# Second attention of a two-block transformer kernel: values held in the array, probabilities scaled before they are transposed

## The chip, the cores and the metric

One core of a Trainium2 chip runs the whole program. The metric is the device time in microseconds (us), the median of several executions. The engines are PE (matrix multiply, with its weight loads listed as PEld), DVE, ACT and POOL (elementwise work) and SP (issues the weight DMAs). Each takes its own instructions strictly in the order of the program, and they meet only through semaphores.

## The reference, cut to what matters

Two transformer blocks run one after the other on 256 tokens of width 1024, all in float32. The change touches only the attention of the second block. It has four mixers of four heads each, with a head size of 64: `moba`, `nsa` (three branches: compressed, selected `slc`, windowed `win`), `diff` (`df1`, `df2`) and `swa`. With 256 tokens every one of them comes down to masked maps of 256 x 256:

```python
s = q @ k.T * scale - slope * dist          # masked, per head
p = exp(s - max) / sum                      # swa adds a sink to the sum
o = p @ v                                   # (256 x 256) @ (256 x 64)
o_nsa = g0 * o_cmp + g1 * o_slc + g2 * o_win
mix = concat([o_moba, o_nsa, o_diff, o_swa])   # 256 x 1024
x = x + rms_norm(mix @ w_out)
```

Of a map only three blocks of 128 x 128 are not masked: query block 0 with key block 0, and query block 1 with both. There are 16 maps of `slc`, `win`, `swa` and `moba`, and 8 of `diff`, which are mixed into 4 before they meet their values. `k` and `v` of nsa are shared by its heads; swa shares each of two pairs between two heads.

## The kernel before, in words

Everything runs as one long list of steps, `ORDER` (line 436), which all five engines walk; each emits its own part of a step and skips what is not its own. A stage's list is made by `weave` (line 188): the string `MIX[...]` says at each place whether the next step comes from the main work ("." takes the next slot of projections) or from one of the side jobs (a letter takes the next step of that job). The stage of this change is `MIX["maps"]` (lines 429 and 430). Its main work is fourteen projection tiles in two halves each (`gemm`, 12 matmuls of 256 columns a half) and at the end four `down` steps of the output projection `out2` (12 matmuls of 512 columns each); after it come the `tail` steps, the rest of that projection. Weights arrive as float32 and are split into a high and a low part (`split`): the high part by ACT or DVE, the low part by DVE or POOL, as the string `MADE` says.

The side jobs are made from `two` (line 366), one per pair of maps (a group: for instance `("win", 0)` is heads 0 and 1):

- `scores`: PE, both maps of the pair, into two banks of PSUM that are kept until both maps are read;
- `score` (one map): DVE adds the bias, writes the scores to an SBUF buffer of the ring `ringP` and takes the extreme of each row;
- `exp` (one map): ACT, with the row sums;
- `p_turn` (one map): PE transposes the three blocks (line 1293), ACT copies them to a buffer of `ringT`, and DVE takes the reciprocal of the row sums, times the gate for nsa (line 2139);
- `value` (one map): PE, with the transposed probabilities stationary and the 64 columns of the values moving (`apart`, line 900: two column halves of the array, each 64 output rows, side by side);
- `o_out` (one map): DVE multiplies the result by the reciprocal, row by row, into `OM2`, which holds tokens in rows and features in columns; `win` adds onto `slc`.

`cmp_value` (two steps) multiplies the compressed probabilities with their values and DVE adds them in. `OM2` is then turned into what the output projection takes, features in rows: `join` (eight steps, line 1311) has PE transpose two blocks, ACT write the high part of the operand `mi` and DVE the low part.

The banks of PSUM for side jobs form a ring of five (`B5`); a step that takes a bank waits until its last reader is through. `ringP` has 7 buffers and `ringT` 5. Free order matters: a `p_turn` of PE needs `exp` alone, and `value` needs ACT's copy of the transposed block.

Of the kernel before, what the change touches and what calls it, by code (L numbers as in the profile page):

```python
# [21 lines left out]
NUNREAD = 13  # L22
NBASE = 4
# [190 lines left out]
def segments():  # L214
# [151 lines left out]
    def two(g):  # L366

        a, b = GROUPS[g]
        return [("scores", g), ("score", a), ("exp", a), ("score", b), ("exp", b), ("p_turn", a), ("value", a), ("p_turn", b), ("o_out", a),
                ("value", b), ("o_out", b)]  # L370

    for n in range(2):
        jobs.append(two(("slc", n)) + two(("win", n)) + [("cmp_value", n), ("join", 2 + n)])
# [4 lines left out]
    for n in range(2):  # L378
        jobs.append(two(("swa", n)) + ([("join", 6), ("join", 7)] if n else []))
    for n in range(2):  # L380
        jobs.append(two(("moba", n)) + [("join", n)])
# [27 lines left out]
    def names(steps):  # L409
# [19 lines left out]
    "maps": "...a.....acbabcbc..cc.bbb.ede.eed.ecag.agcdgcggadc.b.bfcgbefdc.ab.dgfbe.dbhffbbhhhfa.ccccf.igecbeif."  # L429
            "gahf.ddib.b.bbigchijbjj..cbhcibchkhajkhcikkhcjbiijbcijkijkcijg.kjjkk.ggkkij.k.",  # L430
# [27 lines left out]
LAST_JOIN = [s for s in ORDER if s[0] == "join"][-1]  # L458
# [124 lines left out]
def program(nc, dr):  # L583
    ctx = ExitStack()
    with ctx:  # L585
# [184 lines left out]
        OM2 = fa(o, 2048).rearrange("p (c n) -> p c n", c=2); o += 2048  # L770
        PcT, VC = fa(o, 256), fa(o + 256, 256); o += 512
        ringP = [fa(o + 384 * i, 384) for i in range(7)]; o += 7 * 384
        ringT = [fa(o + 384 * i, 384) for i in range(5)]; o += 5 * 384
# [30 lines left out]
        HEAD = dict(moba=0, slc=4, win=4, df1=8, swa=12)  # L804
# [13 lines left out]
        for m, i in p_slot.items():  # L818
            p_prior[m] = at_p.get(i - 7)
        for m, i in t_slot.items():  # L820
            t_prior[m] = at_t.get(i - 5)
# [8 lines left out]
        def Pm(m):  # L830
            return ringP[p_slot[m] % 7]

        def Tm(m):
            return ringT[t_slot[m] % 5]
# [23 lines left out]
        def opened(e, u):  # L858
# [6 lines left out]
            elif PLACE[u] >= NBASE and OPENS[1] <= u < OPENS[1] + NWIDE - NBASE:  # L865
                e.wait_ge(*pe.at(LAST_JOIN))

# [14 lines left out]
        def tensor(e):  # L882
# [53 lines left out]
            for step in ORDER:  # L936
# [356 lines left out]
                elif kind == "p_turn":  # L1293
# [3 lines left out]
                    e.wait_ge(*(dve.at(("d_mix", m_[1])) if m_[0] == "df1" else act.at(("exp", m_))))  # L1297
# [3 lines left out]
                elif kind == "value":  # L1301
# [8 lines left out]
                    apart(b[:, 64:128], PT[:, 256:384], V[1], start=False).then_inc(*pe.up(step))  # L1310
                elif kind == "join":
# [4 lines left out]
                    for c in range(2):  # L1316
                        m = e.transpose(b[:, 128 * c:128 * c + 128], OM2[:, c, 128 * kt:128 * kt + 128], ident)
# [15 lines left out]
                elif kind in ("o_out", "d_out"):  # L1333
                    banks.give(("value", a[0] if kind == "o_out" else ("df1", a[0])))
# [18 lines left out]
                elif kind == "cmp_turn":  # L1353
# [4 lines left out]
                    m.then_inc(*pe.up(step))  # L1358
                elif kind == "cmp_value":
                    n, = a  # L1360
                    b = bank(step, B5)
                    e.wait_ge(*act.at("cmp_turn"))
                    e.wait_ge(*dve.at("cmp_kv"))
                    for c in range(2):
                        m = e.matmul(b[:, 128 * c:128 * c + 128], PcT[:, 128 * c:128 * c + 128], VC[:, 128 * n:128 * n + 128],
                                     start=True, stop=True)
# [3 lines left out]
        def scalar(e):  # L1370
# [3 lines left out]
            for step in ORDER:  # L1374
# [268 lines left out]
                elif kind == "p_turn":  # L1643
                    m_, = a
                    e.wait_ge(*pe.at(step))
                    if t_prior[m_]:
                        e.wait_ge(*pe.at(("value", t_prior[m_])))
                    e.activation(Tm(m_), banks.of(step)[:, 0:384], ACT.Copy).then_inc(*act.up(step))
                    banks.ended(step, act.now())
                elif kind == "d_out":  # L1650
# [3 lines left out]
                    for c in range(2):  # L1654
                        e.activation(OM2[:, c, 64 * (8 + h):64 * (8 + h) + 64], b[:, 64 * c:64 * c + 64], ACT.Square,
# [33 lines left out]
        def vector(e):  # L1689
# [10 lines left out]
            for step in ORDER:  # L1700
# [438 lines left out]
                elif kind == "p_turn" and a[0][0] != "df1":  # L2139
                    m_, = a  # L2140
                    r = stat(("r", m_), 2)
# [349 lines left out]
```

## Time and profile before

| what | value |
|---|---|
| median of 3 runs | 897.89 us (897.86 to 898.0) |
| the profiled execution | 897.94 us |
| its span, first to last instruction | 896.1 us |
| granted TensorE clock, mean | 0.999 |
| PE busy | 884.4 us (99%) |
| DVE, ACT, POOL busy | 667.4, 466.3, 200.4 us |

The profiled execution's own time is 1.8 us over its span. "Busy" counts the time in which at least one instruction of the engine runs. A row of a timeline gives the start, the busy time, the engine, what it wrote from what, shapes, and how many instructions were merged; the start of the next row less the start of this one is what the row took of PE's time. The arrow in brackets names the engine and tile whose end let the row start. The stage `maps` lies from 519.8 to about 608 us.

### The profile page before, as it was taken

The numbers are of one execution on the slowest core, as the hardware profiler recorded it, in microseconds if no ns is written. First come the engines' busy times: TensorE is split into PE (matmuls) and PEld (weight loads), VectorE is DVE, ScalarE is ACT, GpSimd is POOL, SyncE is SP. The second block draws the span as 40 slices with busy tenths as digits, with TensorE's granted clock in tenths as the row PEclk, the third lists the DMA queues.
The fourth block names the chain that finished last, engine by engine and source line by source line (L and its number), as shares of the span: only waits on it lengthen the run. The fifth ranks groups of instructions, "written<-read, shape, count | busy, mean of one in ns | idle before, by whom it ended". The sixth has DMA issues, their size and how long they took to land.

```text
span 896.1 us, 16529 instructions
## 1 busy us (share of the span) xinstructions
PE 884.4 (99%) x6641; PEld 782.7 (87%) x6641; DVE 667.4 (74%) x1253; ACT 466.3 (52%) x940; POOL 200.4 (22%) x113
## 2 busy tenths in 40 slices
PE   9999999999999999999999999999999999999997
PEld 8879999989999798888888899977888888888886
DVE  7745987586447877786666767768888788788885
ACT  7444336665344774444444657866553545543443
POOL 4123421531132120553214522230001111210100
PEclk9999999999999999999999999999999999999999
DMA  8356453153424746555564374215354465465441
GB/s 331 114 184 234 140 174 112 48 212 142 142 96 145 278 163 236 188 196 187 187 219 169 124 247 165 97 48 211 142 222 161 182 213 204 152 230 188 174 156 48
DMA packets 23180, 153.66 MB, mean 171 GB/s; under 512 B 2864, under 2 KB 3248, under 8 KB 5568
## 3 DMA queue, kind: packets, MB, share of 16 engines
q1 hardware_dynamic: 22384, 150.44, 46.8%
q0 software_dynamic: 576, 2.10, 0.6%
q8 instruction: 53, 0.87, 0.4%
q14 instruction: 23, 0.19, 0.1%
q10 hardware_dynamic: 144, 0.07, 0.0%
HBM read 151.28 MB, written 1.05 MB: 170 GB/s over the span
## 4 chain that ended last, share of the span: by engine, by line
PE 96%; DVE 2%; ACT 1%; issue 1%; DVEq 0%; ACTq 0%
PE pb L528 94%; PE pb L531 2%; ACT FA L534 1%; DVE FA L537 0%; DVE wl L537 0%; ACT R L534 0%; DVE X L543 0%; DVE wh L552 0%; DVE FA L546 0%; ACT wh L534 0%; DVE FA L540 0%; DVE st L540 0%; DVE st L555 0%; DVEq L585 0%; DVE FA L543 0%
## 5 line engine op out<-in xcount | busy, mean ns | idle before, releaser
L528 PE MATMUL pb<-R,wh 128*128 128x256 f32 (+2 forms) x2224 | 545.5, 325 | 3.3 <-DVE R L543 2.0
L528 PE MATMUL pb<-R,wl 128*128 128x256 f32 (+1 forms) x1512 | 420.0, 281 | 0.0
L528 PEld LDWEIGHTS pb<-R,wh 128*128 128x128 f32 x2224 | 369.5, 188 | 43.3 <-ACT R L534 3.4
L537 DVE TENSOR_TENSOR wl<-raw,wh 128x1024 fp32r<-128x1024 f32 (+1 forms) x207 | 273.3, 1344 | 76.6 <-ACT wh L534 74.8
L537 POOL TENSOR_TENSOR wl<-raw,wh 128x1024 fp32r<-128x1024 f32 (+1 forms) x71 | 173.4, 2445 | 581.5 <-ACT wh L534 427.4
L528 PEld LDWEIGHTS pb<-R,wl 128*128 128x128 f32 x1512 | 283.4, 188 | 1.7
L534 ACT ACTIVATE wh<-raw 128x1024 fp32r<-128x1024 f32 (+1 forms) x223 | 226.1, 1044 | 52.0 <-PE pb L528 36.9
L528 PE MATMUL pb<-wh,R 128*128 128x512 f32 (+1 forms) x704 | 227.1, 389 | 0.1
L528 PEld LDWEIGHTS pb<-wh,R 128*128 128x128 f32 x704 | 131.7, 188 | 31.1 <-issue 1.7
L534 ACT ACTIVATE FA<-pb 128x256 f32<-128x256 f32 (+7 forms) x240 | 93.2, 411 | 118.4 <-PE pb L528 103.2
L528 PE MATMUL pb<-wl,R 128*128 128x512 f32 (+1 forms) x352 | 135.5, 385 | 0.0
L534 ACT ACTIVATE FA<-FA 128x256 f32<-128x256 f32 (+4 forms) x69 | 28.0, 406 | 138.9 <-DVE FA L543 118.8
L537 DVE TENSOR_TENSOR FA<-FA 128x256 f32<-128x256 f32 (+7 forms) x120 | 71.6, 621 | 10.1 <-ACT FA L534 2.9
L528 PEld LDWEIGHTS pb<-wl,R 128*128 128x128 f32 x352 | 66.1, 188 | 11.6
L537 DVE TENSOR_TENSOR FA<-pb,FA 128x256 f32<-128x256 f32 (+1 forms) x132 | 56.5, 434 | 24.8 <-ACT FA L534 24.3
L534 ACT ACTIVATE R<-FA 128x256 fp32r<-128x256 f32 (+1 forms) x66 | 28.3, 431 | 52.2 <-DVE FA L537 52.2
L528 PE MATMUL pb<-FA 128*32 128x16 f32 (+6 forms) x1360 | 54.0, 217 | 0.3 <-ACT FA L534 0.2
L528 PEld LDWEIGHTS pb<-FA 128*32 128x32 f32 (+3 forms) x1360 | 47.1, 130 | 7.2 <-issue 2.0
L552 DVE CAST wh<-raw 128x1024 fp32r<-128x1024 f32 (+1 forms) x55 | 42.3, 771 | 13.3 <-PE pb L528 12.7
L537 DVE TENSOR_TENSOR R<-FA,R 128x256 fp32r<-128x256 f32 (+1 forms) x59 | 27.4, 468 | 26.2 <-ACT R L534 26.1
L543 DVE SCALAR_TENSOR_TENSOR FA<-FA,sm 128x255 f32<-128x255 f32 x64 | 31.0, 484 | 2.3
L534 ACT ACTIVATE FA<-FA,st 128x256 f32<-128x256 f32 (+2 forms) x65 | 29.3, 454 | 5.2 <-DVE st L546 4.9
(127 smaller groups left out, 434.6 us busy)
## 6 DMA issues: line engine op xcount, KB each, us to landing
raw<-in_w SPq DMA_DIRECT2D x137, 1024.0 KB, 4.8
X<-in_x SPq DMA_DIRECT2D x2, 512.0 KB, 4.1
raw<-in_w SPq DMA_DIRECT2D x2, 512.0 KB, 6.8
post<-in_ffn_post SPq DMA_DIRECT2D x2, 512.0 KB, 4.3
post<-in_w POOLq DMA_DIRECT2D x2, 512.0 KB, 4.9
FA<-in_w POOLq DMA_DIRECT2D x2, 512.0 KB, 8.0
out<-X SPq DMA_DIRECT2D x4, 256.0 KB, 2.0
cst<-in_cst SPq DMA_DIRECT2D x1, 822.5 KB, 12.6
```

What stands on the lines that cost most here:

```text
L528: return self.real.matmul(*a, **k) if self.real else self
L531: return self.real.transpose(*a, **k) if self.real else self
L534: return self.real.activation(*a, **k) if self.real else self
L537: return self.real.tensor_tensor(*a, **k) if self.real else self
L543: return self.real.scalar_tensor_tensor(*a, **k) if self.real else self
L552: return self.real.tensor_copy(*a, **k) if self.real else self
```

## The change

It changes how the 16 maps of `slc`, `win`, `swa` and `moba` meet their values; `diff` stays as it was.

1. A new step `scale` per pair: DVE takes the reciprocals of both maps (with sink and gate), then multiplies the exponentials in SBUF by them: both parts (128 and 256 columns) of the first map and the 128 columns of the second on DVE, the 256 columns of the second on POOL.
2. `p_turn` waits for the scaled map, no longer for `exp` alone, and both maps of a pair are transposed before
3. one step `values` per pair: the values (128 x 64) are stationary, one head in each column half of the array, and the transposed probabilities move, 256 columns for key block 0 and 128 for key block 1. The result has features in rows. For `win` the compressed branch goes into the same bank first, as one matmul of 256 columns, so the two `cmp_value` steps go.
4. `o_out` per pair writes the operand `mi` straight from PSUM: ACT the high part, DVE the low part. `slc` is copied to SBUF by ACT; `win` adds it on DVE, then ACT writes the high part and DVE the low part; `swa` is written in two halves of 64 rows each. Six of the eight `join` steps go (those of `diff` stay).
5. `ringP` has 12 buffers instead of 7, `ringT` 7 instead of 5; `OM2` shrinks.
6. The string `MIX["maps"]` loses the letters of the steps that went, with a few letters moved.

```diff
@@ two(g)
-        return [("scores", g), ("score", a), ("exp", a), ("score", b), ("exp", b), ("p_turn", a), ("value", a), ("p_turn", b), ("o_out", a),
-                ("value", b), ("o_out", b)]
+        return [("scores", g), ("score", a), ("exp", a), ("score", b), ("exp", b), ("scale", g), ("p_turn", a), ("p_turn", b), ("values", g),
+                ("o_out", g)]
@@ MIX
-    "maps": "...a.....acbabcbc..cc.bbb.ede.eed.ecag.agcdgcggadc.b.bfcgbefdc.ab.dgfbe.dbhffbbhhhfa.ccccf.igecbeif."
-            "gahf.ddib.b.bbigchijbjj..cbhcibchkhajkhcikkhcjbiijbcijkijkcijg.kjjkk.ggkkij.k.",
+    "maps": "...a.....acbabcbc..cc.bbb.ede.eed.ecag.agcdgcggad.b.bfcgefdc.ab.dgfbe.dbhffbbhhhfa.ccccf.igecbeif."
+            "gahf.ddib.b.babigchijjj..cbhcibhkjkhcikkhcjijijkijkg.kjjk.ggkk..",
@@ tensor
+                elif kind == "values":
+                    g, = a
+                    b = bank(step, B5, True)
+                    for m_ in GROUPS[g]:
+                        e.wait_ge(*act.at(("p_turn", m_)))
...
+                    if g[0] == "win":
...
+                        e.matmul(b[:, 0:256], VC[:, 128 * g[1]:128 * g[1] + 128], PcT, start=True, stop=False)
+                    for c, t, k in ((0, slice(0, 256), slice(0, 256)), (1, slice(128, 256), slice(256, 384))):
+                        for m_ in GROUPS[g]:
+                            j = 64 * (m_[1] % 2)
+                            m = e.matmul(b[j:j + 64, t], MAPS[m_]["v"][c], Tm(m_)[:, k], start=c == 0 and g[0] != "win", stop=c == 1)
+                    m.then_inc(*pe.up(step))
@@ scalar
+                elif kind == "o_out":
+                    (name, n), = a
+                    b = banks.of(("values", a[0]))
+                    e.wait_ge(*pe.at(("values", a[0])))
+                    if name == "slc":
+                        e.activation(SLC[n], b[:, 0:256], ACT.Copy).then_inc(*act.up(step))
+                        banks.ended(("values", a[0]), act.now())
+                    elif name == "win":
+                        e.wait_ge(*dve.at(("sum", n)))
+                        e.activation(operand("mi", 2 + n, 0), SLC[n], ACT.Copy).then_inc(*act.up(("mi", "h", 2 + n)))
+                    elif name == "moba":
+                        e.activation(operand("mi", n, 0), b[:, 0:256], ACT.Copy).then_inc(*act.up(("mi", "h", n)))
+                    else:
+                        for _, h in GROUPS[a[0]]:
+                            j = slice(64 * (h % 2), 64 * (h % 2) + 64)
+                            e.activation(operand("mi", 6 + h // 2, 0)[j, :], b[j, 0:256],
+                                         ACT.Copy).then_inc(*act.up(("mi", "h", 6 + h // 2), ("swa_h", h)))
@@ vector
+                elif kind == "scale":
+                    for m_ in GROUPS[a[0]]:
...
+                        e.reciprocal(r, stat(("sum", m_), 2)).then_inc(*dve.up())
...
+                    for m_ in GROUPS[a[0]]:
+                        S = Pm(m_)
+                        e.wait_ge(*dve.at(("r", m_)))
+                        for c in range(2 if m_ == GROUPS[a[0]][0] else 1):
+                            e.tensor_scalar(S[:, cols[c]], S[:, cols[c]], stat(("r", m_), 2)[:, c:c + 1], None,
+                                            ALU.mult).then_inc(*dve.up(("scaled", m_)))
...
+                    if name == "win":
+                        e.wait_ge(*act.at(("o_out", ("slc", n))))
+                        e.wait_ge(*pe.at(("values", a[0])))
+                        e.tensor_tensor(SLC[n], b[:, 0:256], SLC[n], ALU.add).then_inc(*dve.up(("sum", n)))
...
+                    elif name == "swa":
+                        for _, h in GROUPS[a[0]]:
+                            j = slice(64 * (h % 2), 64 * (h % 2) + 64)
+                            e.wait_ge(*act.at(("swa_h", h)))
+                            e.tensor_tensor(operand("mi", 6 + h // 2, 1)[j, :], b[j, 0:256], rf(operand("mi", 6 + h // 2, 0)[j, :]),
+                                            ALU.subtract).then_inc(*dve.up(("mi", "l", 6 + h // 2)))
@@ gpsimd
+                elif kind == "scale":
+                    m_ = GROUPS[a[0]][1]
+                    S = Pm(m_)
+                    e.wait_ge(*dve.at(("r", m_)))
+                    e.tensor_scalar(S[:, cols[1]], S[:, cols[1]], stat(("r", m_), 2)[:, 1:2], None, ALU.mult).then_inc(
+                        *pool.up(("scaled", m_)))
```

By the new string, the steps between the last projection half (`mk` 1) and the first `down` are: p_turn win 2; values win 0; p_turn swa 0; p_turn win 3; scale swa pair 1; o_out win 0; p_turn swa 3; scores moba 1; score moba 1; score moba 2; values swa 0; values win 1; p_turn swa 2; exp moba 2; score moba 3; o_out swa 0; o_out win 1; exp moba 1; p_turn swa 1; scale moba 0; values swa 1; p_turn moba 0; exp moba 3; o_out swa 1; p_turn moba 1; scale moba 1; d_norm. (After `p_turn`, `exp` and `score` the number is the head's, after the others the pair's.)

## Rows read from the trace of the kernel before

**Rows 1.** The page: busy time of the engines; the chain that ended last, by engine.
```profile
PE 884.4 (99%) x6641; PEld 782.7 (87%) x6641; DVE 667.4 (74%) x1253; ACT 466.3 (52%) x940; POOL 200.4 (22%) x113
...
PE 96%; DVE 2%; ACT 1%; issue 1%; DVEq 0%; ACTq 0%
```

**Rows 2.** Timeline of PE, 573 to 576 us: one `value` between projections.
```profile
573.95 0.57 PE L528 MATMUL pb<-FA 128*64 128x64 f32 x12
574.45 0.50 PE L528 MATMUL pb<-R,wh 128*128 128x256 f32 x2
...
575.97 0.49 PE L531 MATMUL pb<-cst,FA 128*128 128x128 f32 x3
```

**Rows 3.** Timeline of PE, 583 to 594 us: from the last projection to the first `down`.
```profile
583.41 1.27 PE L528 MATMUL pb<-FA 128*64 128x64 f32 x36
584.61 0.55 PE L531 MATMUL pb<-cst,FA 128*128 128x128 f32 x3
585.74 0.87 PE L531 MATMUL pb<-cst,FA 128*128 128x128 f32 x6 [0.58 <-ACT FA L534]
...
592.66 1.31 PE L531 MATMUL pb<-cst,FA 128*128 128x128 f32 x10
593.72 0.48 PE L528 MATMUL pb<-wh,R 128*128 128x512 f32 x1
```

**Rows 4.** Timeline of PE, 173 to 175 us: 256 moving columns over four column quarters.
```profile
173.50 1.07 PE L528 MATMUL pb<-FA,cst 128*32 128x256 f32 x16
174.50 0.52 PE L528 MATMUL pb<-R,wh 128*128 128x272 f32 x2
```

**Rows 5.** Timeline of ACT, 588 to 595 us: two `exp`, copies of transposed blocks, operand copies.
```profile
588.62 0.40 ACT L534 ACTIVATE FA<-FA,st 128x128 f32<-128x128 f32 x1
...
589.51 0.39 ACT L534 ACTIVATE FA<-FA,st 128x128 f32<-128x128 f32 x1
...
590.39 0.85 ACT L534 ACTIVATE FA<-pb 128x384 f32<-128x384 f32 x2
...
591.13 0.39 ACT L534 ACTIVATE R<-pb 128x256 fp32r<-128x256 f32 x1
...
594.00 0.67 ACT L534 ACTIVATE R<-pb 128x256 fp32r<-128x256 f32 x2
```

**Rows 6.** Groups of DVE by shape, 539 to 625 us: busy us, mean ns of one.
```profile
L540 DVE TENSOR_SCALAR FA<-pb,st 128x64 f32<-128x64 f32 x24 | 5.6, 277 | 0.2 <-PE pb L528 0.2
...
L537 DVE TENSOR_TENSOR R<-pb,R 128x256 fp32r<-128x256 f32 x8 | 3.1, 419 | 4.5 <-ACT R L534 4.5
...
L540 DVE TENSOR_SCALAR FA<-FA,st 128x256 f32<-128x256 f32 x4 | 1.4, 349 | 0.0
...
L540 DVE TENSOR_SCALAR FA<-FA,st 128x128 f32<-128x128 f32 x4 | 1.1, 283 | 0.0
```

**Rows 7.** Timeline of POOL, 545 to 600 us.
```profile
561.98 0.85 POOL L540 TENSOR_SCALAR FA<-cst 128x256 f32<-128x256 f32 x1 [10.88 <-DVE st L546]
...
583.32 4.68 POOL L537 TENSOR_TENSOR wl<-raw,wh 128x1024 fp32r<-128x1024 f32 x2 [9.58 <-ACT wh L534]
```

**Rows 8.** Timeline of DVE, 574 to 578 us: a split, `d_out`, the first reciprocal of win 0.
```profile
576.08 1.23 DVE L537 TENSOR_TENSOR wl<-raw,wh 128x1024 fp32r<-128x1024 f32 x1
577.22 0.35 DVE L543 SCALAR_TENSOR_TENSOR FA<-pb,sm 128x64 f32<-128x64 f32 x2
577.49 0.15 DVE L555 RECIPROCAL st<-st 128x2 f32<-128x2 f32 x1
```

**Rows 9.** Timelines of PE, 1 to 10 and 618 to 623 us: its first matmuls; its longest wait.
```profile
1.44 5.73 PE L528 MATMUL pb<-R 128*128 128x512 f32 x13 [1.44 <-DVE st L564]
...
618.33 0.62 PE L528 MATMUL pb<-wh,R 128*128 128x512 f32 x2
...
619.01 0.39 PE L528 MATMUL pb<-wh,R 128*128 128x512 f32 x1
...
621.38 1.83 PE L528 MATMUL pb<-R,wh 128*128 128x256 f32 x14 [1.11 <-DVE R L543]
```

More of the change, by code:

```diff
@@ L22 @@
 NUNREAD = 13
+NTURN = 7
+NPROB = 12
 NBASE = 4
@@ L368, in two @@
         a, b = GROUPS[g]
-        return [("scores", g), ("score", a), ("exp", a), ("score", b), ("exp", b), ("p_turn", a), ("value", a), ("p_turn", b), ("o_out", a),
-                ("value", b), ("o_out", b)]
+        return [("scores", g), ("score", a), ("exp", a), ("score", b), ("exp", b), ("scale", g), ("p_turn", a), ("p_turn", b), ("values", g),
+                ("o_out", g)]
     for n in range(2):
-        jobs.append(two(("slc", n)) + two(("win", n)) + [("cmp_value", n), ("join", 2 + n)])
+        jobs.append(two(("slc", n)) + two(("win", n)))
     for h in range(4):
@@ L378, in segments @@
     for n in range(2):
-        jobs.append(two(("swa", n)) + ([("join", 6), ("join", 7)] if n else []))
+        jobs.append(two(("swa", n)))
     for n in range(2):
-        jobs.append(two(("moba", n)) + [("join", n)])
+        jobs.append(two(("moba", n)))
     segs.append(("maps", p.take(), jobs))
@@ L457 @@
     TAIL_AT.update({(_n, _k): BLOCK_AT["tail", _n] + 8 * _i for _i, _k in enumerate(_ks)})
-LAST_JOIN = [s for s in ORDER if s[0] == "join"][-1]
+LAST_READ = [s for s in ORDER if s[0] in ("join", "values")][-1]
 class Sig:
@@ L803, in program @@
                                   vs="tm2_out", sink=sc("sinks", h), less_sink=stat("less_sink", 4)[:, h:h + 1])
-        HEAD = dict(moba=0, slc=4, win=4, df1=8, swa=12)
+        KTILE = dict(moba=0, win=2, swa=6)
         def bias_of(m):
@@ L830, in Pm, with multiplied @@
         def Pm(m):
-            return ringP[p_slot[m] % 7]
+            return ringP[p_slot[m] % NPROB]
         def Tm(m):
-            return ringT[t_slot[m] % 5]
+            return ringT[t_slot[m] % NTURN]
+        def multiplied(m):
+            return ("value", m) if m[0] == "df1" else ("values", GROUP_OF[m][0])
         ALL = (0, 1, 2, 3, 4, 5, 6, 7)
@@ L865, in opened @@
             elif PLACE[u] >= NBASE and OPENS[1] <= u < OPENS[1] + NWIDE - NBASE:
-                e.wait_ge(*pe.at(LAST_JOIN))
+                e.wait_ge(*pe.at(LAST_READ))
+                e.wait_ge(*dve.at(("o_out", ("win", 0))))
+                e.wait_ge(*dve.at(("o_out", ("win", 1))))
         FOLDED = ("g1", "u1", "g2", "u2")
@@ L1333, in tensor @@
                 elif kind in ("o_out", "d_out"):
-                    banks.give(("value", a[0] if kind == "o_out" else ("df1", a[0])))
+                    banks.give(("values", a[0]) if kind == "o_out" else ("value", ("df1", a[0])))
                 elif kind == "cmp_act":
@@ L1357, in tensor @@
                         m = e.transpose(b[:, 128 * c:128 * c + 128], Sc_[:, 128 * c:128 * c + 128], ident)
[L1358 to L1366, printed above, removed]
                     m.then_inc(*pe.up(step))
```

93 lines of the change are left out of this document (44 added, 49 removed).

## The prediction

> **What bounds the kernel now.** I read the page's busy times first, then its chain: PE is busy for 99% of the span and is 96% of the chain that ended last [rows 1]. So the time is PE's own work plus PE's waits, and any other engine counts only where PE waits for it. The timeline of PE gives both: the start of a row less the start of the one before is what it took. In this stage PE is not quite full. Three transposes from 584.61 should take 0.33 us and the next row starts 1.13 us later, with 0.58 us marked as a wait for ACT [rows 3]. Between 583.41 and 593.72, 10.3 us, PE does side jobs only, and there its order of steps depends on ACT and DVE without projections between them as cover. That is the stretch to watch.
>
> **PE's own work.** *Joins.* Ten transposes take 593.72 - 592.66 = 1.06 us [rows 3], 0.11 each. Six joins of two go: -1.3 us. *Values.* A `value` alone takes 574.45 - 573.95 = 0.50 us for 12 records [rows 2], three in a row 584.61 - 583.41 = 1.20 us for 36 [rows 3]. So each is 0.35 us and each visit to the column halves costs 0.15 us beside it. Sixteen are 5.6 us. A `values` step has per half a matmul of 256 and one of 128 columns, each in two passes (12 records for six matmuls in rows 2 show the two). No trace has 256 columns in two halves. Where four column quarters take 256 columns each, sixteen records take 174.50 - 173.50 = 1.00 us [rows 4]; less the visit, four rounds of 0.22 us. With halves side by side like that, `values` is 2 x 0.22 + 2 x 0.11 = 0.65 us; if they ran one after the other it would be 1.3 us. I take 0.65, since the 64-column halves of rows 2 and the quarters of rows 4 both run side by side. Eight are 5.2 us: -0.4 us. *Compressed branch.* Two `cmp_value` of four records of 0.11 (0.9 us) become four records of 0.22 (0.9 us): nothing. *Visits.* Ten runs of values become eight, and transposes stand together more: about -0.5 us. In all -2.2 us. The transposes of the maps stay as they are.
>
> **DVE, ACT, POOL.** DVE loses 32 multiplications out of PSUM, 5.6 / 24 = 0.23 us each [rows 6], 7.5 us, and gains per pair two of 128 and one of 256 columns; by the busy time of their rows, 1.1 / 4 and 1.4 / 4 us [rows 6], that is up to 0.9 us, back to back about 0.65, or 5 to 7 us in all. ACT gains two copies for `slc` and two for the halves of `swa`, 0.34 us each [rows 5]; 64 rows instead of 128 may cost the same or half. I take the same, as the time goes with the columns in these rows. POOL gains eight of 0.85 us [rows 7], and two pairs stand behind two splits of 4.68 us together [rows 7]. These loads are small, and none of them bounds. What matters is order.
>
> **Waits added.** `p_turn` waited for `exp`; now it waits for DVE and POOL behind it. And `o_out` now bounces: for `win` DVE adds, ACT copies, DVE subtracts; for `swa` ACT copies twice, DVE subtracts twice. Each bounce holds whatever is queued behind it on both engines. I walked the four queues through the stage in the order of the steps, each with the durations of the rows, an operation starting when its queue is free and 0.05 us after its last producer, banks and ring buffers included. For the kernel before, the walk puts the end of the last projection at 583.5 and the first `down` at 593.6, where the rows have 583.41 and 593.72 [rows 3], with 3.4 us of PE waits in the stage. So I trust it to some tenths. For the changed order it gives three places.
>
> 1. *Up to the last projection, +0.6 us.* Work -1.5, waits +2.1. The largest: `p_turn` win 0. DVE got to its first reciprocal at 577.49 [rows 8], since a split to 577.22 and a `d_out` stand ahead. Before, nobody waited for that. Now four dependent small operations (0.27 each pair), then 0.45 us of scaling come first: ready at 578.4 or later, while PE arrives two projection halves after 574.45, at 577.5. With a shift of 0.7 us inherited from ACT and DVE, where `exp` of diff now stands behind the later `p_turn` slc 2, PE waits 1.4 us. That shift itself costs 0.6 us at `p_turn` df1 0.
> 2. *From the last projection to the first `down`, +3.5 us.* PE's work there falls from 8.5 to 7.9 us. Waits rise from 1.5 to 5.7 us. The first two, 0.6 and 0.75 us, are banks: `p_turn` swa 3 takes one whose ACT copy stands behind the splits, and `values` swa 0 one that `score` moba 1 frees, which DVE reaches only after the bounce of win 0. The third decides everything: `values` swa pair 1 needs ACT's copy of `p_turn` swa 1. On ACT's queue, after PE has finished `p_turn` swa 2, stand: its copy (0.37), `exp` moba 2 (589.51 - 588.62 = 0.89), two operand copies for swa 0 (0.67), the copy for win 1, `exp` moba 1 (0.88), the copy wanted (0.48 to its end) [rows 5]. The copy for win 1 waits for DVE, which first subtracts the two swa halves and then adds, three operations of 3.1 / 8 = 0.39 us at most, 0.34 back to back [rows 6], counted from the first swa copy: ACT stands for 1.0 us. Sum: 0.37 + 0.89 + 0.67 + 1.0 + 0.3 + 0.88 + 0.48 = 4.6 us. In it PE has only `p_turn` swa 1, 0.33 us. PE waits 4.3 us there. In the old order the same `exp` moba 1 was released by DVE's plain multiplications and PE had eight more short steps in between.
> 3. *The four `down` and after, +0.2 us.* `p_turn` moba 2 now stands behind the first `down` and waits 0.3 us for its scaling. The chains after the tails hang on PE's last `tail` and shift with it.
>
> The sum: -2.2 of work, +6.5 of waits (9.9 against 3.4) = +4.3 us. On the profiled execution, 897.94 us, that is 902.2 us; the median stands 0.05 us lower, which makes no difference. If the copies of 64 rows cost half, ACT's queue in place 2 is 0.3 us shorter, and scaling at its upper end makes place 1 longer by 0.2: small beside the rest.
>
> **Rivals.** *A: the waits are hidden, faster.* One place decides: whether `values` swa 1 starts right after `p_turn` swa 1, because ACT has its copy ready. If PE waits there under 1 us, and the rest of the queues keep their old slack, the sum is the work alone, -2.2, and up to 1.5 us of the old waits go too, since fewer banks are taken (eight instead of sixteen, and eight steps gone). 894.3 to 895.7 us, say 895.7. For it: the page shows ACT at 52% and DVE at 74% [rows 1], `ringP` gets five more buffers, and the old dense stretch got by with 1.5 us of waits. Against it: the order on ACT's queue is written in the string and can't overlap.
>
> *B: the halves don't run side by side at 256 columns.* 8 x 0.65 = 5.2 us more, about 4 of it on the path: 906.3 us. Rows 2 and 4 speak against it.
>
> *C: the clock falls.* PE's first 13 matmuls of 512 columns, straight after its first wait, took 5.73 us, 0.44 each, while three of the same width take 619.01 - 618.33 = 0.68 us, 0.23 each, once it runs [rows 9]: the lower of its two levels (1.2 GHz) against the upper. The longest wait that PE has had since is marked with 1.11 us [rows 9], and the granted clock held through it. A wait of 4.3 us is beyond what this trace shows. If the clock fell and came back after a stretch as at the start, the price is 13 x (0.44 - 0.23) = 2.7 us on top: 904.9 us. The Trainium skill, page TensorE: Matmul & The Clock Gate (Part 1, the HAM clock gate), says that an idle PE is taken back to half its clock and has to earn it again; by that rule 904.9 is a possible outcome here, and no row of this trace shows such a fall.
>
> *D: half way.* The big wait is there but shorter, because ACT gets to `exp` moba 1 earlier than I think (for instance DVE's add comes before the swa subtractions are waited for): 897 to 900.5 us.
>
> **Chances.** Forecast (901 to 904) 0.54, A 0.18, B 0.04, C 0.09, D 0.15. About 0.2%, 1.8 us, is what a measurement of this kernel can tell from no change. D splits into 0.09 within it and 0.06 slower; so slower 0.73, same 0.09, faster 0.18. The range 896.0 to 905.5 takes in D and C and leaves out B and most of A; the forecast's own is 901 to 904.
>
> **What would show it.** In the profile after: a `values` step without the compressed part should take about 0.8 us from start to start (0.65 and a visit), 1.4 or more would mean B. The timeline of PE should have one wait of 4 us just before a group of 128 x 64 records with 256 columns, between the last projection and the first `down`, with ACT as releaser, and on ACT's timeline two `exp` and two or three `R<-pb` copies in that time, with a gap of about 1 us before a copy that reads SBUF. It should also show a wait of 1 to 1.5 us before the transposes behind the last but one projection tile. PE's busy time should fall by about 2 us. A granted clock under 0.99 would be C. If PE's longest wait in the stage is under 1.5 us, my walk is wrong and A holds.

## The result, and the profile after

The changed kernel takes 909.28 us (median of 4 runs, 907.98 to 910.19), the kernel before 897.94 us on the same chip: a ratio of 1.0124, 95% interval 1.0111 to 1.0136. It is slower, as forecast, but by 11.3 us where I had said 4.3, and outside my range. The profiled execution took 909.21 us, its span 907.4.

The page of the changed kernel, first the busy times, then the rows of PE and of its granted clock over 40 slices of 22.7 us, then its chain:

```profile
PE 886.0 (98%) x6497; PEld 780.7 (86%) x6497; DVE 671.3 (74%) x1247; ACT 466.9 (51%) x944; POOL 209.5 (23%) x121
...
PE   9999999999999999999999999969999999999997
...
PEclk9999999999999999999999999979999999999999
...
PE 91%; DVE 4%; ACT 3%; issue 1%; DMA 1%; SPq 0%; DVEq 0%
```

PE has 144 records fewer and yet is 1.6 us longer busy than in [rows 1]. One slice, the one around 600 us, is short of work and of clock (its digits are 6 and 7 where the rest have 9). Its timeline of PE, from the last projection to the second `down`:

```profile
585.27 0.49 PE L533 MATMUL pb<-cst,FA 128*128 128x128 f32 x3
...
588.68 0.94 PE L530 MATMUL pb<-keys,FA 64*128 64x128 f32 x12
592.20 3.89 PE L530 MATMUL pb<-FA 128*64 128x256 f32 x18 [2.58 <-DVE st L548]
...
601.58 1.55 PE L530 MATMUL pb<-FA 128*64 128x256 f32 x8 [4.69 <-DVE FA L542]
...
604.25 0.78 PE L530 MATMUL pb<-wh,R 128*128 128x512 f32 x1
...
608.35 0.87 PE L530 MATMUL pb<-FA 128*64 128x256 f32 x8
609.15 0.55 PE L533 MATMUL pb<-cst,FA 128*128 128x128 f32 x3
```

The projections end at 585.27 (583.41 in [rows 3]) and the first `down` starts at 604.25 (593.72). So 1.9 us are lost up to the end of the last projection, 8.7 us between it and the first `down`, and 0.7 us behind. The two `values` of swa are the rows at 592.20 (with `values` win 1 merged in) and 601.58. The stretch in the windows view (columns: window, its length, busy us and instructions of PE, PEld, DVE, ACT and POOL, granted clock, DMA share, GB/s):

```profile
592.20:596.00 3.80, 3.80 (x18) 1.95 (x18) 1.05 (x8) 0.00 (x0) 0.18 (x1) 0.55 0.81 276
...
601.58:604.25 2.67, 2.67 (x14) 2.01 (x15) 0.32 (x1) 0.26 (x1) 0.69 (x1) 0.50 0.00 0
604.25:606.00 1.75, 1.75 (x6) 1.46 (x5) 0.34 (x1) 1.73 (x7) 0.00 (x0) 0.50 0.00 0
```

In these windows, behind the two long waits, the granted clock is at its lower level (1.2 GHz): 0.55 and 0.50 instead of 1.00. That was my rival C, and it comes on top of the forecast. The sign that I had set for it, a granted clock under 0.99 for the whole run, did not show: the mean is 0.994 (0.999 before), since the falls are short against 907 us. It has to be looked for behind the waits.

What held the first wait stands in the timelines of DVE and POOL:

```profile
589.31 2.28 DVE L539 TENSOR_TENSOR R<-FA,R 128x256 fp32r<-128x256 f32 x1 [1.84 <-ACT R L536]
591.51 0.28 DVE L548 CUSTOM_DVE_ANT_0 FA<-pb,FA 128x128 f32<-128x128 f32 x1
...
600.15 0.43 DVE L539 TENSOR_TENSOR R<-FA,R 128x256 fp32r<-128x256 f32 x1 [0.55 <-ACT R L536]
```
```profile
586.64 4.66 POOL L539 TENSOR_TENSOR wl<-raw,wh 128x1024 fp32r<-128x1024 f32 x2 [2.24 <-ACT wh L536]
```

The subtraction for win pair 0 takes 2.28 us, the same for win pair 1, with POOL idle, 0.43. It ends 0.3 us after POOL's two splits (586.64 + 4.66 = 591.30). Both of its operands lie in SBUF. `score` moba 1, which frees the bank of `values` swa 0, stands behind it. The trace of before had the pattern already, and I had not looked for it (DVE, then POOL; at 1.23 us each, as in [rows 8], the two splits would take 2.4 us):

```profile
700.33 3.72 DVE L537 TENSOR_TENSOR wl<-raw,wh 128x1024 fp32r<-128x1024 f32 x2 [1.47 <-ACT wh L534]
```
```profile
699.43 2.40 POOL L537 TENSOR_TENSOR wl<-raw,wh 128x1024 fp32r<-128x1024 f32 x1 [3.58 <-ACT wh L534]
```

The Trainium skill, page SBUF — State Buffer (Who interferes with whom), says that a DVE operation with two inputs in SBUF contends with an operation of POOL that reads SBUF, under an exclusive lock. By that rule the subtraction costs what is left of POOL's split on top of its own time, and the trace agrees (it ends 0.3 us behind the split). I had not weighed that rule.

The second wait is the one that I worked out. ACT's timeline, from the end of `p_turn` swa 2:

```profile
596.60 0.49 ACT L536 ACTIVATE FA<-pb 128x384 f32<-128x384 f32 x1 [7.01 <-PE pb L533]
...
597.87 0.77 ACT L536 ACTIVATE R<-pb 64x256 fp32r<-64x256 f32 x2
599.63 0.42 ACT L536 ACTIVATE R<-FA 128x256 fp32r<-128x256 f32 x1 [0.99 <-DVE FA L539]
599.95 0.39 ACT L536 ACTIVATE FA<-FA,st 128x128 f32<-128x128 f32 x1
...
600.94 0.49 ACT L536 ACTIVATE FA<-pb 128x384 f32<-128x384 f32 x1
```

Copy, `exp` moba 2, two copies for swa 0, a stand of 0.99 us (I had 1.0), the copy for win 1, `exp` moba 1, and at 600.94 the copy that is wanted: the chain of place 2 of the prediction, operation by operation. PE's row names a DVE operation as its releaser; in the code `values` swa 1 waits for ACT's copies, and the last of them ends at 601.43. So here the name in the brackets is another's.

### The profile page after: what moved, and what is told of

Read it like the earlier page. It is cut to its first block, busy times and chain, and to the rows that moved or that the text cites. A ratio compares the mean times of both kernels' runs of the same rounds, so it can differ in the third digit from the quotient of the medians.

```text
span 907.4 us, 16255 instructions
## 1 busy us (share of the span) xinstructions
PE 886.0 (98%) x6497; PEld 780.7 (86%) x6497; DVE 671.3 (74%) x1247; ACT 466.9 (51%) x944; POOL 209.5 (23%) x121
## 4 chain that ended last, share of the span: by engine, by line
PE 91%; DVE 4%; ACT 3%; issue 1%; DMA 1%; SPq 0%; DVEq 0%
PE pb L530 90%; ACT FA L536 2%; PE pb L533 2%; DVE wl L539 1%; DMA sm<-in_sm 1%; DVE FA L548 1%; DVE FA L542 1%; ACT wh L536 1%; DVE FA L539 0%; ACT R L536 0%; DVE wh L554 0%; DVE st L557 0%; SPq L569 0%; DVE st L539 0%; DVE X L545 0%
## 5 line engine op out<-in xcount | busy, mean ns | idle before, releaser
L536 ACT ACTIVATE FA<-pb 128x256 f32<-128x256 f32 (+8 forms) x242 | 93.9, 412 | 129.7 <-PE pb L530 106.3
L530 PE MATMUL pb<-FA 128*32 128x16 f32 (+10 forms) x1228 | 55.0, 225 | 8.3 <-DVE FA L542 4.7
L530 PEld LDWEIGHTS pb<-FA 128*32 128x32 f32 (+3 forms) x1228 | 45.0, 131 | 17.2 <-DVE FA L542 4.9
L539 DVE TENSOR_TENSOR R<-FA,R 128x256 fp32r<-128x256 f32 (+1 forms) x61 | 30.1, 497 | 28.6 <-ACT R L536 28.5
```

Source lines behind the costliest of these rows:

```text
L530: return self.real.matmul(*a, **k) if self.real else self
L536: return self.real.activation(*a, **k) if self.real else self
L539: return self.real.tensor_tensor(*a, **k) if self.real else self
```

## The experiments

All times are medians, ratios are against the kernel before on the same chip (898.1 to 898.2 us there). "The changed kernel" is 909.28 us.

**The sum of win kept in PSUM.** DVE's low part then reads one operand from PSUM.

```diff
-  e.tensor_tensor(SLC[n], b[:, 0:256], SLC[n], ALU.add)
+  e.tensor_tensor(b[:, 0:256], b[:, 0:256], SLC[n], ALU.add)
-  e.activation(operand("mi", 2 + n, 0), SLC[n], ACT.Copy)
+  e.activation(operand("mi", 2 + n, 0), b[:, 0:256], ACT.Copy)
-  e.tensor_tensor(operand("mi", 2 + n, 1), SLC[n], rf(operand("mi", 2 + n, 0)), ALU.subtract)
+  e.tensor_tensor(operand("mi", 2 + n, 1), b[:, 0:256], rf(operand("mi", 2 + n, 0)), ALU.subtract)
```

> One edit to the changed kernel: for win, DVE adds the slc part onto the values in their own PSUM bank (instead of into the SBUF copy), ACT's high part and DVE's low part read that bank. Theory (a collision): in the changed kernel's trace DVE's subtraction for win pair 0 took 2.28 us instead of 0.43, and it ended 0.3 us after POOL's split that was running; it reads two operands in SBUF, and the two engines do not do that side by side. Reading PSUM it takes 0.42 us again, the bank for `values` swa 0 comes free 1.9 us earlier, PE's wait there falls from 2.6 to about 0.8 us, the granted clock does not fall behind it (1.7 us more). The wait of 4.7 us before `values` swa 1 stays, with its fall of the clock. In all about 3.6 us less than the changed kernel: 905.7 us. Rival (the bounce itself holds DVE: it waits for ACT's copy behind the splits): the subtraction starts at the same point and PE's wait stays at 2.6 us, 909.3 us.

905.35 us, ratio 1.0083 (1.0069 to 1.0097). Its DVE, and POOL beside it:

```profile
589.10 0.42 DVE L539 TENSOR_TENSOR R<-pb,R 128x256 fp32r<-128x256 f32 x1 [1.80 <-ACT R L536]
```
```profile
586.46 4.68 POOL L539 TENSOR_TENSOR wl<-raw,wh 128x1024 fp32r<-128x1024 f32 x2 [2.23 <-ACT wh L536]
```

The same subtraction, started under the same split of POOL, takes 0.42 us. The collision is shown. The edit gives 3.9 us. That is more than the 1.9 us of the subtraction, because the clock now stays up through the first stretch (1.00 from 592 to 596 us) and is down for a shorter time behind the second wait. PE now waits 1.01 us before the scores of moba pair 1, since the bank of win is held longer.

**Two steps moved ahead.** `cikkhcjij` in the string becomes `cikkjihcj`.

> One edit to the changed kernel: in the string of `maps`, exp moba 1 and p_turn swa 1 come ahead of o_out swa 0 and o_out win 1 instead of behind them. Theory (the third wait is the sum of what stands ahead of ACT's copy for p_turn swa 1): two operand copies, the copy for win and its stand for DVE no longer come first, so PE's wait before `values` swa 1 falls from 4.7 to about 2.7 us. But the scaling of moba pair 0 then stands behind the bounces on DVE, and PE waits 1.7 to 2.3 us before `p_turn` moba 0. So most of it only moves: 907.5 to 909 us. Rival (the wait is due to something that the order does not touch, as the scaling of swa pair 1 or a bank): the wait stays at 4.7 us before `values` swa 1.

909.32 us, ratio 1.0127 (1.0113 to 1.0140). PE's rows:

```profile
599.67 0.87 PE L530 MATMUL pb<-FA 128*64 128x256 f32 x8 [2.15 <-ACT FA L536]
603.15 1.09 PE L533 MATMUL pb<-cst,FA 128*128 128x128 f32 x4 [2.62 <-DVE FA L542]
```

The time is the changed kernel's own, 0.3 us above the range that I had given. The wait of 4.69 us falls to 2.15, and one of 2.62 comes up before `p_turn` moba 0. So the order makes the wait, and this order only moves it.

**PE's waits filled with idle work.** Matmuls on the identity, whose result nobody reads, ahead of the two `values` of swa. The first length was wrong: 22 and 38 matmuls, which are 44 and 76 records and took 5.1 and 8.6 us. The edit is shown with the second length, 11 and 18.

```diff
+  if g[0] == "swa":
+      f = bank(("fill", g[1]), (0, 1, 2))
+      for _ in range(11 if g[1] == 0 else 18):
+          e.matmul(f[:, 0:128], ident, ident, start=True, stop=True)
```

> One edit to the changed kernel: PE does idle work in two of its waits, 22 matmuls of 128 columns on the identity into a bank that nobody reads before `values` swa 0 and 38 before `values` swa 1 (0.11 us each, so 2.4 and 4.2 us of the waits of 2.6 and 4.7 us). The order and all waits stay. Theory (the clock): in the changed kernel the granted clock is at the lower level from 592.2 to about 595 and from 601.6 to 606.0 us, behind the two waits; with PE at work it stays at the upper level, and the kernel is 3.2 to 3.7 us faster, 905.6 to 906.1 us. Rival (the slow rows are due to reads or banks, or the time is set by ACT and DVE through that stretch): no gain, 909.3 us or more.

912.61 us, ratio 1.0161 (1.0147 to 1.0174): it tells nothing of the price, as the fill itself ran over the waits. With the second length:

> The fill of PE's two waits once more, with its length put right: in the first such kernel one matmul of 128 columns on the identity took 0.23 us, not 0.11, so that 5.1 and 8.6 us of idle work ran over both waits by 2.3 and 4 us. Now 11 before `values` swa 0 (2.55 us of a wait of 2.7) and 18 before `values` swa 1 (4.2 us of a wait of 4.5). The order and all waits stay those of the changed kernel. Theory (the clock costs 1.7 + 1.2 + 0.8 us behind the two waits): the granted clock stays at the upper level through the stretch and the time is 905.5 to 906.2 us, the waits keeping their length. Rival (the rows are slow for another reason, or ACT and DVE set the time through the stretch): 909 us.

905.75 us, ratio 1.0086 (1.0072 to 1.0100). Windows and PE's rows of that run:

```profile
592.20:596.00 3.80, 3.80 (x33) 3.15 (x32) 0.38 (x3) 1.77 (x7) 0.00 (x0) 1.00 0.57 237
...
599.20:600.60 1.40, 1.40 (x14) 1.14 (x15) 0.30 (x1) 0.04 (x1) 0.67 (x1) 1.00 0.00 0
```
```profile
588.74 2.72 PE L530 MATMUL pb<-cst 128*128 128x128 f32 x22
591.39 2.30 PE L530 MATMUL pb<-FA 128*64 128x256 f32 x18
593.62 0.88 PE L533 MATMUL pb<-cst,FA 128*128 128x128 f32 x6
594.33 4.18 PE L530 MATMUL pb<-cst 128*128 128x128 f32 x36
599.18 0.87 PE L530 MATMUL pb<-FA 128*64 128x256 f32 x8 [0.67 <-DVE FA L542]
...
600.61 0.47 PE L530 MATMUL pb<-wh,R 128*128 128x512 f32 x1
...
604.16 0.55 PE L533 MATMUL pb<-cst,FA 128*128 128x128 f32 x3 [0.55 <-DVE FA L542]
```

The waits, now with the fill in them, have kept their length and the clock is full. The 18 records from `values` swa 0 on take 593.62 - 591.39 = 2.2 us, in the changed kernel 596.02 - 592.20 = 3.8; from `values` swa 1 to `down` 1.4 against 2.7. The first `down` takes 0.75 us longer in the changed kernel (607.93 - 604.25 = 3.68 us) than in the kernel before (596.65 - 593.72 = 2.93 us). Slow rows so cost 1.6 + 1.2 + 0.75 = 3.6 us. With the clock up, a wait of 0.55 us that the slow `down` had covered comes up before `p_turn` moba 2 (the row at 604.16), so by these rows the net price is 3.0 us; the medians differ by 3.5 us, and the four executions of the changed kernel differ among themselves by up to 2.2 us. The clock's price is 3.0 to 3.5 us.

**One letter j stands 12 places earlier.**

```diff
-  cbhcibhkjkhcikkhcjij
+  cbhcijbhkjkhcikkhcij
```

> One edit to the changed kernel: one letter j of the string of `maps` stands 12 places earlier, so that score moba 1 comes ahead of o_out win 0 (it was behind it) and exp moba 1 ahead of exp moba 2 and the two o_out (it was behind them). Theory (order of the two queues): the bank that `values` swa 0 takes is freed before DVE goes into the bounce of win 0, so the wait of 2.6 us falls to about 0.6 with the collision still there; the wait before `values` swa 1 falls from 4.7 to about 3.2 us, since one exp less stands ahead. The clock falls at most once. The walk of the queues gives 5.5 us less than the changed kernel: 903.8 us. Rival (ACT has too much to do in this stretch, order does not matter): the wait moves to another step and the time stays within 1 us of 909.3.

903.94 us, ratio 1.0067 (1.0055 to 1.0080). PE's rows:

```profile
589.82 2.30 PE L530 MATMUL pb<-FA 128*64 128x256 f32 x18 [0.55 <-ACT FA L536]
...
596.74 1.55 PE L530 MATMUL pb<-FA 128*64 128x256 f32 x8 [3.60 <-DVE st L557]
```

One letter gives back 5.3 of the 11.3 us. The collision is still in this kernel (DVE's subtraction takes 2.29 us at 589.39), but PE does not wait for it.

**No scaling.** The step `scale` is left out on DVE and POOL, and `p_turn` waits for `exp`. This kernel leaves out the division by the sums, the gates and the sink; it serves for its time alone.

> The changed kernel with the step `scale` left out (the probabilities are not multiplied by the reciprocal, gate and sink; everything else is computed) and `p_turn` waiting for `exp` alone as in the kernel before. Theory (the scaling is a small part of the loss, in place 1): the 1.4-us wait before `p_turn` win 0 goes, and so does the shift before cmp_hid 1; waits of 2 us and 4.3 us before `values` swa 0 and 1 stay, since the bounces of o_out make them. The walk of the queues gives 4.4 us less than the changed kernel, 904.9 us. Rival (the scaling makes most of the loss): 899 us or less, and no wait over 1.5 us.

905.26 us, ratio 1.0075 (1.0063 to 1.0088). The waits of 1.74 and 4.68 us before the two `values` of swa are there:

```profile
588.29 2.30 PE L530 MATMUL pb<-FA 128*64 128x256 f32 x18 [1.74 <-DVE st L548]
...
596.08 1.55 PE L530 MATMUL pb<-FA 128*64 128x256 f32 x8 [4.68 <-ACT FA L536]
```

So scaling costs 4.0 us, some of it through the clock, which stays up behind the wait of 1.74 us; without it the kernel is still 7 us slower than before. That the bounces of `o_out` make most of this rest is read from the chains above; no run takes the bounces away.

**New orders for the whole stage.** A search over moves of letters, priced by the walk of the queues. First over the whole string, for both kernels:

> The kernel before with another order of the same steps: the string of `maps` found by a search over moves of letters with the walk of the queues. No computation changes. The walk takes the waits of the stage from 3.4 to 0.3 us and one or two visits away, 4.4 us less: 893.5 us. It is the comparison for the changed kernel in an order of its own. Rival (the waits of this stage are already as short as the weights' arrival allows): 897 to 899 us.

906.88 us, ratio 1.0092 (1.0077 to 1.0107).

> The changed kernel with another order of the same steps, found by the same search: nothing else is changed. The walk of the queues has 0.35 us of PE waits in the stage in place of 11, no wait long enough for the clock to fall, and the scores of late pairs under the projections. 16.6 us less than the changed kernel: 892.7 us, under the kernel before and about 1 us under that kernel in its own new order, as PE's work is 2.2 us less but for some more visits. Rival (the loss is in the steps themselves, not in their order): above 905 us. Between them lies what the walk leaves out, the arrival of weights above all, as this order runs six projection halves without a pause at its start.

906.16 us, ratio 1.0089 (1.0075 to 1.0103). Both missed by 13 us. In both PE waits 3.8 us for a transfer, and the clock is down behind it (0.50 from 550 to 560 us in the changed kernel). PE of the changed kernel:

```profile
548.50 0.64 PE L530 MATMUL pb<-post,CQ 128*32 128x128 f32 x16 [3.76 <-DMA post<-in_w]
```

That is not the whole miss: the kernel before also waits 3.60 us at 594 and the changed one 2.02 us at 580, each with a fall of the clock, and I have not added these up. The weights of cmp_hid 2 are loaded where those of cmp_hid 0 lay, and arrive some 10 us after its use, which the new orders put late. The walk had no transfers. With this one in it, and the first 50 letters kept:

> The changed kernel with another order of the same steps from cmp_act on (the first 50 letters of the string and the last 12 stay, as the search before let PE wait 4.2 us for the weights of cmp_hid, whose transfers start only once the earlier half is used). The walk, with that transfer in it, has 2.2 us of PE waits in the stage, none over 0.7 us, so the clock holds: 14.2 us less in the walk, 895.0 us. Rival (the loss lies in the steps and comes back as other waits): above 903.9 us, the best so far.

897.06 us, ratio 0.9987 (0.9979 to 0.9996).

> The changed kernel with the win sum kept in PSUM, so that DVE's low part does not read two operands in SBUF, and its own new order of the steps from cmp_act on. The walk has 1.6 us of PE waits: 894.5 us. If the collision no longer matters once the order gives it cover, it is the same as the one without this edit to 0.5 us.

901.85 us, ratio 1.0039 (1.0027 to 1.0051).

> The kernel before with another order of its steps from cmp_act on, found by the same search under the same limits; no computation changes. The walk has 0.4 us of PE waits in place of 3.4, and 3.7 us less in all: 894.3 us. By it the change itself, each kernel in its best order, is worth nothing (its 2.2 us less of work for PE go into visits and into waits that the longer chains make). Rival (the change is worth its 2.2 us once its waits are hidden): this kernel is at 896.5 us or more and 2 us behind the changed one in its order.

895.87 us, ratio 0.9975 (0.9966 to 0.9985).

> The changed kernel with another order from the projection of swa on alone (the first 97 letters stay). The walk has 3.5 us of waits, those of the first part, and 12.2 us less in all: 896.7 us. Against the kernel with the longer reordering it tells what the waits of the first part cost (1.6 us in the walk).

899.54 us, ratio 1.0011 (1.0003 to 1.0020). The first of these orders of the changed kernel takes back 12.2 us by order alone. The first and the last of the changed kernel missed the walk by 2.1 and 2.8 us, the kernel before in its order by 1.6. The one with the sum in PSUM missed by 7.4 us and spreads from 898.39 to 904.31. Its profiled execution (900.22 us) has waits of 1.19 and 2.20 us that the walk does not have, and the clock at its lower level behind the first; the rest of this miss stays open. In the first (DVE, then POOL), as PE waits 1.20 us, there is a collision again:

```profile
596.93 3.52 DVE L542 TENSOR_SCALAR FA<-FA 128x64 f32<-128x64 f32 x8
```
```profile
597.68 2.39 POOL L539 TENSOR_TENSOR wl<-raw,wh 128x1024 fp32r<-128x1024 f32 x1 [3.08 <-ACT wh L536]
```

The kernel before takes 1.39 us for these eight. Each has one tensor operand (and one factor per row), so the collision is not one of two-operand instructions alone. With it in the walk for more of DVE's operations:

> The changed kernel in one more order of the same steps from cmp_act on. The run with the first such order had four waits that the walk did not have (0.8, 0.7, 0.6 and 1.2 us); the last stood behind the normalisation of diff, whose eight small DVE operations took 3.52 us instead of 1.3 while POOL had a split. This order comes from the same search with that collision in the walk for every DVE operation that reads and writes SBUF alone. Walk: 1.6 us of waits, 895.6 us by the offset of the first such order. Theory (the 3 us of waits are the whole difference between PE's work and the time): 895 to 896 us, level with the kernel before in its order (895.9) or just under it. Rival (the waits come back elsewhere): 897 us or more.

901.35 us, ratio 1.0037 (1.0025 to 1.0050): the rival.

> The changed kernel with an order of the steps that is new from the 21st letter on, so that the steps around cmp_hid and the first scores of slc move too, where every run of the changed kernel so far waits 0.8 us (the scaling of slc pair 0 stands ahead of a split and of the scores on DVE). The walk has this wait gone and 0.9 us at p_turn moba 3 in its place: 895.4 us. Rival (the transfers of cmp_hid's weights, which this order may start later, cost more than is gained): 898 us or more, with a wait marked for a DMA.

898.70 us, ratio 1.0006 (0.9997 to 1.0015): no wait for a DMA, but one of 3.35 us behind the same eight operations, 3.55 us long here. In the run before it, DVE's chain of the compressed probabilities stood, which my walk had let pass (DVE, POOL, PE):

```profile
584.24 1.96 DVE L542 TENSOR_SCALAR st<-st 128x8 f32<-128x8 f32 x1
586.23 0.20 DVE L557 RECIPROCAL st<-st 128x8 f32<-128x8 f32 x1
586.47 2.02 DVE L539 TENSOR_TENSOR st<-st,FA 128x8 f32<-128x8 f32 x1
```
```profile
583.81 4.66 POOL L539 TENSOR_TENSOR wl<-raw,wh 128x1024 fp32r<-128x1024 f32 x2
```
```profile
588.87 0.66 PE L533 MATMUL pb<-cst,FA 128*128 128x128 f32 x2 [2.89 <-DVE FA L539]
```

Eight columns, 2 us, for two of the operations; the reciprocal between them takes 0.20 us with POOL's second split running. The test is to take POOL's two splits away (`p` to `d` at two places of `MADE`):

> The last order but one of the changed kernel (it took 901.35 us), with one edit: the low parts of two weight splits, which POOL made in 4.66 us just before PE's wait of 2.9 us, are made by DVE. Theory (collision): in that run a DVE operation on 128 x 8 elements took 2.02 us and the one before it 1.96, each until POOL's split ended. Though DVE now has 2.3 us more work just there, the chain of the compressed probabilities no longer stands, PE's wait of 2.9 us falls under 0.6, the clock holds, and the time is 895.6 us. Rival (DVE is short of time there and the long operations are a matter of the record): with 2.3 us more on DVE the wait grows, 902 us or more.

897.83 us, ratio 0.9995 (0.9987 to 1.0004), 3.5 us less. Its DVE:

```profile
586.77 0.17 DVE L539 TENSOR_TENSOR st<-st,FA 128x8 f32<-128x8 f32 x1
```

2.02 us has become 0.17, with more work on DVE. That PE's wait went with it shows the collision as its cause; that 2 us less were gained than expected stays open in part: PE has waits of 0.87 and 0.83 us near 570 there, as in the run before, which the walk does not have. Last, two orders from a search that counts all this and may move splits:

> The changed kernel with a new order from the 51st letter on and three splits moved between DVE and POOL, from a search whose walk has the collision for all DVE operations that stay in SBUF. Walk: 1.1 us of waits, 611.4, by the offsets of the earlier orders 893.9 to 894.8 us. Theory (work term of 2.2 us holds once nothing waits): under the 895.9 us of the kernel before in its own order. Rival (waits of another kind come up): 896.5 us or more.

894.30 us (893.77 to 894.35), ratio 0.9954 (0.9941 to 0.9966).

> A second result of the same search from another seed, five splits moved: walk 612.0, 894.4 to 895.4 us. Same theory and rival as the one before it; it tells whether such a result is a matter of luck in one order.

898.41 us, ratio 1.0005 (0.9996 to 1.0014): a wait of 1.85 us at 578.6 that the walk did not have. The walk is no fine measure. With the transfer in it, it met one order (894.3 us), missed five by 1.6 to 3.3 us, and two by 5.8 and 7.4. The first of the two is the fastest kernel of this study; besides the string, low parts of two splits go from DVE to POOL and one goes back:

```diff
-    "maps": "...a.....acbabcbc..cc.bbb.ede.eed.ecag.agcdgcggad.b.bfcgefdc.ab.dgfbe.dbhffbbhhhfa.ccccf.igecbeif."
-            "gahf.ddib.b.babigchijjj..cbhcibhkjkhcikkhcjijijkijkg.kjjk.ggkk..",
+    "maps": "...a.....acbabcbc..cc.bbb.ede.eed.ecag.agcdgcggad.gffbdfbf.edaff...ecbcbahhccee.hhdh..gbcdacibbbihfc"
+            ".db.jiihjbi.hfgifcb.gjij.cbkaghjkckkjhibcbiikjkjcg.kjjk.ggkk..",
```

Busy times of the page, first the kernel before in its new order (895.87 us), then this one:

```profile
PE 883.4 (99%) x6641; PEld 782.9 (88%) x6641; DVE 668.8 (75%) x1253; ACT 465.7 (52%) x940; POOL 200.2 (22%) x113
```
```profile
PE 880.7 (99%) x6497; PEld 778.3 (87%) x6497; DVE 671.7 (75%) x1246; ACT 467.0 (52%) x944; POOL 212.3 (24%) x122
```

## Why the prediction was right in direction and wrong in size

- *PE's own work, -2.2 us.* Right. `values` takes 609.15 - 608.35 = 0.80 us from start to start, the 0.65 and a visit of the forecast, so the halves run side by side and rival B is out. With the waits gone, PE is busy for 880.7 us against 883.4 and 884.4 of the two orders of the kernel before: 2.7 to 3.7 us less.
- *Place 1, +0.6 us.* Measured 1.5 us: 585.27 against 583.41, less 0.36 us by which this run came late to the stage (its first projection starts at 520.14, before at 519.78). The wait before `p_turn` win 0 was forecast with 1.4 us and is marked with 1.16; the one at `p_turn` df1 0, forecast with 0.6, is marked with 0.65. The rest is a wait of 0.81 us before the scores of diff 3, behind the first `scale`; on the way to it DVE multiplied 128 x 2 gates in 0.50 us under a split of POOL instead of 0.16. The step cost more than the sum had, and its parts below half a microsecond are not separated.
- *Place 2, +3.5 us.* Measured 8.7. Two steps failed. The bank wait of 0.75 us before `values` swa 0 is 2.58, and the missing 1.9 us is DVE's subtraction standing under POOL's splits, which the walk did not have. And the sum had no term for the clock behind the waits, though it forecast one of 4.3 us: there are 1.6 us of lower clock behind the first long wait and 1.2 behind the second. The chain of the third wait was right (4.3 forecast, 4.69 measured), and the wait at `p_turn` swa 3 is 0.40 us instead of 0.6: 3.5 + 1.9 + 2.8 + 0.4 - 0.2 = 8.4, with 0.3 left open.
- *Place 3, +0.2 us.* Measured 0.7, all of it the first `down` at the lower clock (0.75 us). The wait of 0.3 us at `p_turn` moba 2 is not in this trace, as the slow `down` covers it; with the clock up it is 0.55 us.
- *Rival C had 0.09 and came true, at a price of 3.0 to 3.5 us instead of 2.7.* I priced one fall; there were two, as the collision made a second long wait. The Trainium skill's rule (TensorE: Matmul & The Clock Gate, Part 1) that an idle PE falls to half its clock is borne out by the windows above.
- *Rival A* (waits hidden, 895.7 us) is what the kernel becomes in a suitable order with three splits moved: 894.3 us, and 897.1 us by order alone. So the loss was no property of the change but of the string written for it.

By the sum: 4.3 forecast, 1.9 and about 0.3 for the collision, 3.0 to 3.5 for the clock, 0.4 for the third wait, and the remaining 1 us or so in place 1 and in the start of the run. Collision and clock overlap: either cured alone gives 3.5 to 3.9 us.

What the change itself is worth: 894.3 us is 0.46% under the kernel before and 1.6 us under that kernel in its own new order, 0.9954 (0.9941 to 0.9966) against 0.9975 (0.9966 to 0.9985), two intervals that just touch at 0.9966. The comparison favours the changed kernel: its last search knew the collision and could move splits, and the one for the kernel before did neither. The changed kernel's best by order alone, 897.06 us, is 1.2 us behind the 895.87 us that the same search found for the kernel before. So whether the change gains anything is not settled; PE's 2.7 to 3.7 us less work is what it could gain.

## What to carry to other kernels

Removing work from the bounding engine is worth what the forecast says only if the order of the queues is fitted to the new chains; a bounce between two in-order engines prices everything queued behind it. When an operation is moved from PSUM to SBUF operands, look at what the other elementwise engine does at that moment. And price a wait of several microseconds on PE with the clock behind it, once for every such wait.

## What the runs showed of the hardware that I had not expected

- DVE's additions, subtractions, multiplications and casts from SBUF stand while POOL runs a split (two operands in SBUF), however small they are: 128 x 8 took 2.02 us instead of 0.17, eight of 128 x 64 took 3.52 instead of 1.39. Not every operation in SBUF does: under the same splits a RECIPROCAL took 0.20 us and a TENSOR_REDUCE 0.27, as without them, and one with an operand in PSUM 0.42. It holds for the whole program: in five traces (the kernel before, the changed one, the kernels of 897.06, 901.35 and 894.30 us), 28 additions of 128 x 256 that lay under a split with both operands in SBUF took 1.07 to 1.94 us instead of 0.43, and 86 with one operand in PSUM took 0.41 to 0.43; 13 casts of 128 x 1024 took 1.38 to 2.90 us instead of 0.69. DVE's scaling beside POOL's scaling loses less: in the changed kernel the three operations take 0.72 us with POOL idle (at 585.05), 0.86 with POOL's of 1.06 us over them (at 601.03), and 1.16 at 606.77.
- No single length of wait tells whether the clock falls. It fell behind waits of 2.58 and 3.60 us and with one of 4.69, and stayed up behind single ones of 1.74 and 2.20 (the second in the 901.85-us kernel); but behind one of 2.02 us, in the changed kernel's first whole order (906.16 us), it fell. In one of the new orders (899.54 us) four shorter waits brought it down, here with the windows behind them:

```profile
583.98 0.94 PE L530 MATMUL pb<-keys,FA 64*128 64x128 f32 x12 [0.33 <-ACT keys L536]
586.12 0.44 PE L533 MATMUL pb<-cst,FA 128*128 128x128 f32 x2 [1.20 <-DVE FA L539]
587.18 0.52 PE L533 MATMUL pb<-cst,FA 128*128 128x128 f32 x3 [0.62 <-DVE FA L542]
587.97 0.55 PE L533 MATMUL pb<-cst,FA 128*128 128x128 f32 x3 [0.28 <-DVE st L548]
```
```profile
588.30:590.00 1.70, 1.70 (x9) 0.78 (x8) 0.86 (x8) 1.44 (x6) 1.70 (x1) 0.57 0.00 0
590.00:592.00 2.00, 2.00 (x13) 1.61 (x10) 1.23 (x5) 1.22 (x5) 1.12 (x2) 0.51 0.42 82
```
